# Expert blocks behind nested tests, weights read in 4096-byte runs, unused slots not gathered

## The chip, the cores and the metric

The kernel runs on one core of a Trainium2 chip. The metric is the device time of one execution in microseconds, as a median of three runs. A profile is one further execution of the same program, taken with the hardware profiler.

## The reference

One inference step of a decoder layer: a projection, two token mixers (sparse attention and gated DeltaNet), an output projection with residual, and a mixture of experts. Only the last part matters here. 1024 prompt rows and 8 sample rows each go to two of 32 experts:

```python
logit_in = jnp.take_along_axis(logit_e, grp[:, None, None], axis=1)[:, 0]
top_v, top_i = lax.top_k(logit_in, TOP_K)
weights = (p_top * jax.nn.softmax(top_v, axis=-1)).astype(h.dtype)
expert = grp[:, None] * EXPERTS_PER_GROUP + top_i
...
return (jax.nn.silu(xb @ w_gate[e]) * (xb @ w_up[e])) @ w_down[e]
...
return jnp.zeros((M, D), h.dtype).at[s_tok].add(out[dest] * s_w[:, None])
```

D is 1024, an expert is 512 wide, everything is float32. An expert's three matrices are 2 MB each, so a block of one expert reads 6.29 MB.

## The kernel before, in words

The program is a row of stages, each ended by a barrier of the engines. The three that the change touches are the last but two, the last but one and the last.

**Output projection (`block_out`, lines 2113 to 2256).** Nine tiles of rows, eight of 128 and one of 8. TensorE multiplies by `w_out`, VectorE adds the residual into `x1` and later scales it by the inverse root mean square into `h2` (line 2225), GpSimd multiplies `h2` in place by the gain (line 2256), and SP stores the tile to the DRAM table `h2_rows` (line 2143). `h2` has two buffers. A last row of zeros is stored behind the 1032 rows (line 2166); the stage ends when that has landed.

**Routing (`block_route`).** VectorE and TensorE work out which slot of which block each assignment gets. A block has 96 slots (`SLOTS`) and belongs to one expert. Blocks 0 to 31 are the first blocks of the 32 experts; an expert with over 96 rows has further blocks, numbered from 32. `tokens` holds for each slot of each block the row to gather (the row of zeros, index 1032, for an unused slot) and the row of the sample output to scatter to. The last element of `blocks` is the number n of blocks in use. Meanwhile SP loads the weights of experts 0, 1 and 2.

**Experts (`block_experts`, from line 2447).** Three weight buffers, two row buffers, two output buffers. For a block, GpSimd gathers 96 rows by an indirect DMA (line 2499), TensorE transposes them (line 2557), multiplies by gate and up weights (2567 and 2569), ScalarE and VectorE make the product (2622, 2656, 2658), TensorE transposes it (2575) and multiplies by the down weights (2587 to 2593), ScalarE and VectorE copy the result out of PSUM, and GpSimd adds it to the outputs with two accumulating indirect DMAs (line 2504), one for the prompt output and one for the sample output, each of which drops the slots that are not its own by a bounds check. SP loads the weights of block b (lines 2270 and 2273) once block b-3 has been used. The down projection of a block follows the gate and up projections of the next one. The 32 first blocks are written out. Further blocks run in a loop on each engine, six written-out bodies for each turn, each body behind a test:

```python
with engine.If(n > NE):
    with engine.Fori(0, (MAXBLK - NE) // 6) as i:
        for j in range(6):
            with engine.If(i * 6 + (NE + j) < n):
                each(i * 6 + (NE + j), ...)
```

(MAXBLK - NE) // 6 is 4. In a further block GpSimd copies the slot indices to `f_idx` first (lines 2531 and 2532), because the block's number is only in a register; and it waits for the scatters of a block before it goes on to the next. The weights' rows lie on partitions as row k * 128 + p, so a run in DRAM is one row of 512 floats, 2048 bytes; a row of the down weights has 1024 floats.

Of the kernel before, what the change touches and what calls it, by code (L numbers as in the profile page):

```python
# [17 lines left out]
ALU = mybir.AluOpType  # L18
# [3 lines left out]
P = 128  # L22
D = 1024
KD = D // P
# [21 lines left out]
MAXBLK = 56  # L46
MAXOVER = 24
# [2066 lines left out]
def block_out(nc, L, PS, C, x_p, x_s, norm_ffn, w_rg, w_re, b_rg, b_re, mixed, wo, wo_loaded, h2_rows, logits, y_p, y_s):  # L2114

    ctx = ExitStack()
    with ctx:
# [16 lines left out]
        bias = Z("o_bias", [P, NG + NE])  # L2134
        zrow = Z("o_zero", [1, D])
# [64 lines left out]
        def _(dve):  # L2200
# [10 lines left out]
            for t, n in tiles:  # L2211
# [11 lines left out]
                if t >= 2:  # L2223
                    dve.wait_ge(h2_stored[t % 2], 16 * (t // 2))
# [23 lines left out]
        def _(pool):  # L2248
            pool.wait_ge(small_loaded, 96)
            for t, n in tiles:  # L2250
# [191 lines left out]
def block_experts(nc, L, PS, C, weights, h2_rows, tokens, slot_weight, blocks, y_p, y_s):  # L2442
# [4 lines left out]
    with ctx:  # L2447
# [18 lines left out]
        def further(engine, each):  # L2466

            n = engine.value_load(blocks[0:1, MAXBLK:MAXBLK + 1], min_val=NE, max_val=MAXBLK)
            with engine.If(n > NE):
                with engine.Fori(0, (MAXBLK - NE) // 6) as i:  # L2470
                    for j in range(6):
                        with engine.If(i * 6 + (NE + j) < n):
                            each(i * 6 + (NE + j), (NE + j) % 3, j % 2, i * 2 + (NE + j) // 3 + 1, i * 3 + (NE + j) // 2 + 1)
            return n

        @block.sync
        def _(sp):
# [11 lines left out]
            def each(b, w, par, wu_count, count):  # L2489
                load(b, w, sp.value_load(blocks[0:1, bass.ds(b, 1)], min_val=0, max_val=NE - 1))  # L2490
# [4 lines left out]
        def _(pool):  # L2495
            turn, fetch = pool.alloc_register("turn"), pool.alloc_register("fetch")
# [5 lines left out]
            def scatter(par, index):  # L2502
                for c, y in enumerate((y_p, y_s)):
                    pool.indirect_dma_start(out=y, out_offset=bass.IndirectOffsetOnAxis(ap=index(c), axis=0), in_=out[par][slot, :], in_offset=None,  # L2504
                                            bounds_check=y.shape[0] - 1, oob_is_err=False, compute_op=ALU.add).then_inc(stored[par], 16)

            def scatter_first(b):
# [4 lines left out]
                scatter(b % 2, lambda c: tokens[slot, b, c:c + 1])  # L2512

            gather(0, tokens[slot, 0, 0:1])
            gather(1, tokens[slot, 1, 0:1])
            for b in range(NE):
                pool.wait_ge(xt_done, b + 1)
                gather(b % 2, tokens[slot, b + 2, 0:1])
                if b >= 1:
                    scatter_first(b - 1)  # L2520
            scatter_first(NE - 1)
            pool.wait_ge(stored[1], 32 * (NE // 2))

            def each(b, w, par, w_count, count):

                pool.reg_mov(turn, b + 1)
                done = pool.snap(turn)
                pool.reg_mov(fetch, b - (NE - 1))
                copied = pool.snap(fetch)
                pool.wait_ge(xt_done, done)  # L2530
                nc.gpsimd.tensor_copy(gidx[slot, par, :], tokens[slot, bass.ds(b + 2, 1), :].rearrange("p b c -> p (b c)")).then_inc(gidx_ready, 1)
                nc.gpsimd.tensor_copy(sidx[slot, par, :], tokens[slot, bass.ds(b, 1), :].rearrange("p b c -> p (b c)")).then_inc(sidx_ready, 1)
                pool.wait_ge(xt_done, NE)
                pool.wait_ge(gidx_ready, copied)
                gather(par, gidx[slot, par, 0:1])
                pool.wait_ge(out_act, NE)
                pool.wait_ge(sidx_ready, copied)
                pool.wait_ge(out_act, done)
                pool.wait_ge(out_dve, done)
                scatter(par, lambda c: sidx[slot, par, c:c + 1])  # L2540
                pool.wait_ge(stored[par], count * 32)
                pool.sem_inc(scattered, 1)

            n = further(pool, each)

            pool.wait_ge(x_loaded[0], (n + 1) // 2 * 16 + 16)
            pool.wait_ge(x_loaded[1], n // 2 * 16 + 16)

        @block.tensor
        def _(pe):  # L2550
            def transpose_rows(b, par, count):
                pe.wait_ge(x_loaded[par], 16 * count)
                if not (isinstance(b, int) and b < 1):
# [24 lines left out]
            def down(b, w, w_count):  # L2578
                pe.wait_ge(aT_done, b + 1)
                pe.wait_ge(d_loaded[w], 16 * w_count)  # L2580
                if not (isinstance(b, int) and b < 1):
# [24 lines left out]
            def each(b, w, par, w_count, count):  # L2606
                gate_and_up(b, w, par, w_count)
                transposes(b)
                transpose_rows(b + 2, par, count + 1)
# [169 lines left out]
```

## Time and profile before

| | us |
|---|---|
| median of 3 runs | 2648.46 (2645.39 to 2649.17) |
| the profiled execution | 2640.05 |
| its span | 2638.4 |
| TensorE matmuls busy | 2267.6 (86%) |
| weight loads into TensorE busy | 1623.9 (62%) |
| VectorE, ScalarE, GpSimd busy | 764.0, 508.3, 441.1 |
| DMA | 342.58 MB, mean 130 GB/s |

The span is the time between the first and the last instruction of the profiled execution. The page cuts it into 40 slices of 66 us. Shares are averages over stages with different limits; what the change is worth has to be read from the stage it stands in. PE is TensorE's matmuls, PEld its weight loads, DVE VectorE, ACT ScalarE, POOL GpSimd, SP the engine that issues most DMAs; a q behind a name is that engine's sequencer.

### The profile page before, as it was taken

The numbers are of one execution on the slowest core, as the hardware profiler recorded it, in microseconds if no ns is written. First come the engines' busy times: TensorE is split into PE (matmuls) and PEld (weight loads), VectorE is DVE, ScalarE is ACT, GpSimd is POOL, SyncE is SP. The second block draws the span as 40 slices with busy tenths as digits, with TensorE's granted clock in tenths as the row PEclk, the third lists the DMA queues.
The fourth block names the chain that finished last, engine by engine and source line by source line (L and its number), as shares of the span: only waits on it lengthen the run. The fifth ranks groups of instructions, "written<-read, shape, count | busy, mean of one in ns | idle before, by whom it ended". The sixth has DMA issues, their size and how long they took to land. (4 is left out here: it accounts for less than half of the span.)

```text
span 2638.4 us, 47235 instructions
## 1 busy us (share of the span) xinstructions
PE 2267.6 (86%) x20007; PEld 1623.9 (62%) x20007; DVE 764.0 (29%) x1601; ACT 508.3 (19%) x1413; POOL 441.1 (17%) x515
## 2 busy tenths in 40 slices
PE   8999998997889998798599999995899998998710
PEld 6456755886746655566466666442788787787600
DVE  2016343453656664344200000114111111111100
ACT  2111112331245555332000000101111111111100
POOL 1043121220401112102100000110122121211200
PEclk9999999997689999899699999997899999999965
DMA  5000300001200001754610000225799999999600
GB/s 169 32 32 32 137 2 1 2 2 53 50 1 2 1 1 30 199 153 128 197 47 32 32 32 17 90 80 214 281 371 358 356 368 354 369 351 361 232 13 6
DMA packets 188697, 342.58 MB, mean 130 GB/s; under 512 B 32517, under 2 KB 80142, under 8 KB 188238
## 3 DMA queue, kind: packets, MB, share of 16 engines
q1 hardware_dynamic: 166646, 305.97, 33.1%
q0 software_dynamic: 13632, 26.72, 4.0%
q10 hardware_dynamic: 8160, 6.07, 0.7%
q8 instruction: 208, 3.41, 0.6%
q14 instruction: 51, 0.42, 0.1%
HBM read 316.70 MB, written 44.55 MB: 137 GB/s over the span
## 5 line engine op out<-in xcount | busy, mean ns | idle before, releaser
L2567 PE MATMUL psum<-f_W,f_xT 128*32 128x384 f32 x3264 | 377.0, 506 | 40.2 <-DMA f_W<-w_up 37.2
L2569 PE MATMUL psum<-f_W,f_xT 128*32 128x128 f32 x3264 | 381.6, 281 | 0.1
L2569 PEld LDWEIGHTS psum<-f_W,f_xT 128*32 128x32 f32 x3264 | 365.6, 114 | 4.9 <-issue 0.3
L2083 PE MATMUL psum<-hT,x_wg 128*128 128x344 f32 x768 | 228.4, 456 | 3.3 <-DMA x_wg<-w_in 3.3
L400 PE MATMUL psum<-w,hT 128*128 128x512 f32 (+1 forms) x512 | 202.4, 553 | 0.0
L2083 PEld LDWEIGHTS psum<-hT,x_wg 128*128 128x128 f32 x768 | 147.1, 192 | 80.4 <-DMA x_wg<-w_in 3.4
L2567 PEld LDWEIGHTS psum<-f_W,f_xT 128*32 128x32 f32 x3264 | 148.1, 113 | 45.6 <-issue 37.2
L400 PE MATMUL psum<-hT,w 128*128 128x344 f32 x576 | 169.1, 454 | 0.0
L400 PEld LDWEIGHTS psum<-w,hT 128*128 128x128 f32 x512 | 96.9, 192 | 97.2 <-issue 90.4
L1620 ACT ACTIVATE a_P<-psum,a_nmax 128x512 f32<-128x512 f32 (+4 forms) x256 | 122.9, 494 | 125.1 <-DVE a_nmax L1538 84.9
L400 PEld LDWEIGHTS psum<-hT,w 128*128 128x128 f32 x576 | 108.6, 190 | 57.1 <-ACT dnT L451 0.9
L2656 DVE TENSOR_TENSOR f_a<-f_sg,psum 128x384 f32<-128x384 f32 x34 | 18.8, 554 | 413.1 <-ACT f_sg L2622 413.1
L2587 PE MATMUL psum<-f_W,f_aT 128*32 128x512 f32 x816 | 124.4, 597 | 0.7 <-DVE f_aT L2669 0.7
L2504 POOL DMA_INDIRECT out_y_prompt<-f_out,tokens x32 | 45.6, 1425 | 474.3 <-ACT f_out L2630 453.5
L2589 PE MATMUL psum<-f_W,f_aT 128*32 128x256 f32 x544 | 124.2, 382 | 0.0
L1534 DVE TENSOR_REDUCE a_nmax<-psum 128x2 f32<-128x1024 f32 (+4 forms) x128 | 91.0, 737 | 84.8 <-PE psum L1450 53.8
L2105 DVE TENSOR_TENSOR x_sig<-x_sig,psum 128x344 f32<-128x344 f32 x48 | 22.4, 508 | 318.3 <-ACT x_sig L2098 318.3
L1467 PE MATMUL psum<-constants,a_P 128*128 128x128 f32 (+1 forms) x592 | 94.7, 286 | 1.1 <-DVE a_PT L1517 0.6
L2622 ACT ACTIVATE f_sg<-psum 128x384 f32<-128x384 f32 x34 | 16.7, 490 | 395.5 <-PE psum L2569 395.5
L1447 PE MATMUL psum<-kT,qT 64*128 64x512 f32 (+3 forms) x384 | 83.0, 525 | 7.2 <-ACT a_P L1620 4.9
L2098 ACT ACTIVATE x_sig<-psum 128x344 f32<-128x344 f32 x48 | 19.3, 455 | 318.4 <-PE psum L2088 318.4
L2589 PEld LDWEIGHTS psum<-f_W,f_aT 128*32 128x32 f32 x544 | 60.0, 111 | 33.5 <-issue 0.7
(526 smaller groups left out, 3635.3 us busy)
## 6 DMA issues: line engine op xcount, KB each, us to landing
f_W<-w_gate SPq DMA_DIRECT2D x34, 2048.0 KB
f_W<-w_up SPq DMA_DIRECT2D x34, 2048.0 KB
f_W<-w_down SPq DMA_DIRECT2D x34, 2048.0 KB, 22.6
k_stage<-cache_nsa SPq DMA_DIRECT2D x128, 192.0 KB, 2.5
w<-w_in SPq DMA_DIRECT2D x6, 2048.0 KB, 7.7
x_wg<-w_in SPq DMA_DIRECT2D x8, 1024.0 KB, 10.8
x<-x_prompt SPq DMA_DIRECT2D x8, 512.0 KB, 5.4
o_w<-w_out SPq DMA_DIRECT2D x2, 2048.0 KB
```

Source lines behind the costliest of these rows:

```text
L400: ins = nc.tensor.matmul(PS[i % 4][0:m_rows, 0:n], lhsT, rhs, start=(k == 0), stop=(k == KD - 1))
L1447: ins = nc.tensor.matmul(s[:, g, col:col + w], qT[rows, j, i * P:(i + 1) * P], key, start=True, stop=not masks)
L1467: ins = nc.tensor.transpose(bank[0:keys, x * P:(x + 1) * P], Pb[u % 2][:, g, at:at + keys], C["ident"])
L1534: ins = nc.vector.tensor_reduce(stats[:, c:c + 2], S[n % 2][:, :, col:col + width(part)], AX.X, ALU.max, negate=True)
L1620: ins = nc.scalar.activation(Pb[u % 2][:, g, o:o + w], S[n % 2][:, g, col:col + w], ACT.Exp, bias=nmax[:, u % 2, c0 + g:c0 + g + 1], accum ...
L2083: ins = nc.tensor.matmul(PS[b + i][:, 0:n], wg[q % 3][:, k, i, c:c + P], hT[:, k, t0:t0 + n], start=(k == 0), stop=(k == KD - 1))
L2105: nc.vector.tensor_tensor(sg[u % 2][:, i, 0:n], sg[u % 2][:, i, 0:n], PS[4 * (u % 2) + 2 + i][:, 0:n], ALU.mult).then_inc(t_done, 1)
L2504: pool.indirect_dma_start(out=y, out_offset=bass.IndirectOffsetOnAxis(ap=index(c), axis=0), in_=out[par][slot, :], in_offset=None, bounds_ ...
L2567: nc.tensor.matmul(PS[bank][row[t], 0:NQ], xT[par][:, k, row[t]], m[:, k, 0:NQ], start=(k == 0), stop=(k == KD - 1))
L2569: ins = nc.tensor.matmul(PS[bank][row[3], P * t:P * t + P], xT[par][:, k, row[t]], m[:, k, NQ:FE], start=(k == 0 and t == 0), stop=(k == K ...
L2587: nc.tensor.matmul(PS[5][row[t], :], part(t, k), wd[w][:, k, 0:512], start=(k == 0), stop=(k == 3))
L2589: nc.tensor.matmul(PS[5][row[3], 256 * t:256 * t + 256], part(t, k), wd[w][:, k, 768:D], start=(k == 0 and t == 0), stop=(k == 3 and t == 1))
```

## The change

1. The further blocks are no longer a loop. Blocks 32 to 52 are written out, and the test for each stands inside the body of the test before it, so the first false test leaves all that follow. The block numbers are constants, and the copies of indices, the registers and their semaphores on GpSimd are gone. In a further block GpSimd gathers, scatters, and waits for both before the next block. MAXBLK goes from 56 to 53 and MAXOVER from 24 to 21.
2. Gate and up weights lie on partitions in pairs of rows: partition p gets rows k * 256 + 2p and k * 256 + 2p + 1, which is one run of 4096 bytes. The stored rows `h2_rows` are permuted to match, by GpSimd's multiply, which now reads with a step of two and writes to a buffer of its own, `h2p`. The waits for the stores move with it from VectorE to GpSimd.
3. The gathers have a bounds check: from block 2 on, an unused slot (index 1032) is out of bounds and its row is not fetched. The first two gathers still fetch the row of zeros.

```diff
-MAXBLK = 56
-MAXOVER = 24
+MAXBLK = 53
+MAXOVER = 21
...
+        h2p = Z("o_h2p", [P, 2, D])
+        by_row = lambda x: x.rearrange("p (k j r) -> p k r j", k=KD // 2, r=2)
...
-            sp.dma_start(h2_rows[t * P:t * P + n, :], h2[0:n, t % 2, :]).then_inc(h2_stored[t % 2], 16)
+            sp.dma_start(h2_rows[t * P:t * P + n, :], h2p[0:n, t % 2, :]).then_inc(h2_stored[t % 2], 16)
...
-                    dve.wait_ge(h2_stored[t % 2], 16 * (t // 2))
+                    dve.wait_ge(h2_done, t - 1)
...
-                nc.gpsimd.tensor_tensor(h2[0:n, t % 2, :], h2[0:n, t % 2, :], gain[0:n, :], ALU.mult).then_inc(h2_done, 1)
+                if t >= 2:
+                    pool.wait_ge(h2_stored[t % 2], 16 * (t // 2))
+                nc.gpsimd.tensor_tensor(h2p[0:n, t % 2, :].rearrange("p (k r j) -> p k r j", k=KD // 2, r=2), by_row(h2[0:n, t % 2, :]), by_row(gain[0:n, :]),
+                                        ALU.mult).then_inc(h2_done, 1)
...
-            queue.dma_start(dst, of(w.rearrange("e (k p) n -> e p k n", p=P), e).rearrange("a p k n -> (a p) k n")).then_inc(gu_loaded[i], 16)
+            queue.dma_start(dst.rearrange("p (k r) n -> p k (r n)", r=2), of(w.rearrange("e (k p r) n -> e p k (r n)", p=P, r=2), e).rearrange("a p k n -> (a p) k n")).then_inc(gu_loaded[i], 16)
...
-            with engine.If(n > NE):
-                with engine.Fori(0, (MAXBLK - NE) // 6) as i:
-                    for j in range(6):
-                        with engine.If(i * 6 + (NE + j) < n):
-                            each(i * 6 + (NE + j), (NE + j) % 3, j % 2, i * 2 + (NE + j) // 3 + 1, i * 3 + (NE + j) // 2 + 1)
-            return n
+            with ExitStack() as open_tests:
+                for b in range(NE, MAXBLK):
+                    open_tests.enter_context(engine.If(n > b))
+                    each(b)
...
-            def gather(par, index):
-                pool.indirect_dma_start(out=x[par][slot, :], out_offset=None, in_=h2_rows,
-                                        in_offset=bass.IndirectOffsetOnAxis(ap=index, axis=0)).then_inc(x_loaded[par], 16)
+            def gather(b):
+                pool.indirect_dma_start(out=x[b % 2][slot, :], out_offset=None, in_=h2_rows,
+                                        in_offset=bass.IndirectOffsetOnAxis(ap=tokens[slot, b, 0:1], axis=0),
+                                        bounds_check=TT if b < 2 else TT - 1, oob_is_err=False).then_inc(x_loaded[b % 2], 16)
...
-                nc.gpsimd.tensor_copy(gidx[slot, par, :], tokens[slot, bass.ds(b + 2, 1), :].rearrange("p b c -> p (b c)")).then_inc(gidx_ready, 1)
-                nc.gpsimd.tensor_copy(sidx[slot, par, :], tokens[slot, bass.ds(b, 1), :].rearrange("p b c -> p (b c)")).then_inc(sidx_ready, 1)
...
+            def each(b):
+                pool.wait_ge(xt_done, b + 1)
+                gather(b + 2)
+                scatter(b)
+                pool.wait_ge(stored[b % 2], 32 * (b // 2 + 1))
+                pool.wait_ge(x_loaded[b % 2], 16 * (b // 2 + 2))
```

The other engines' bodies change only in that block numbers and counts are constants.

## Rows read from the trace of the kernel before

**Rows 1.** The page: what the DMA engines moved in each of 40 slices.
```profile
GB/s 169 32 32 32 137 2 1 2 2 53 50 1 2 1 1 30 199 153 128 197 47 32 32 32 17 90 80 214 281 371 358 356 368 354 369 351 361 232 13 6
```

**Rows 2.** Busy time by stretches: length, engines, granted clock, DMA share, GB/s.
```profile
1876.00:1977.00 101.00, 101.00 (x1647) 86.74 (x1645) 17.03 (x34) 12.38 (x27) 19.03 (x15) 1.00 0.96 343
1977.00:2424.00 447.00, 407.90 (x6347) 353.13 (x6350) 70.44 (x142) 54.29 (x119) 89.41 (x71) 0.96 1.02 360
...
2516.20:2638.40 122.20, 0.04 (x3) 0.00 (x0) 0.85 (x2) 1.31 (x3) 2.84 (x2) 0.52 0.05 7
```

**Rows 3.** Chain and timeline: transposes of blocks 0, 6 and 31 (start, us).
```profile
1875.32 0.55 PE psum L2575 x3
...
1977.02 0.48 PE psum L2575 x3
...
2458.93 0.55 PE L2575 MATMUL psum<-constants,f_a 128*128 128x128 f32 x3
```

**Rows 4.** PE's waits, 1860 to 2460 us: total, times, longest.
```profile
PE psum L2567 <- DMA f_W<-w_up: 37.2, 16, 4.0
```

**Rows 5.** SP's last load (start, us), and its wait (total, times, longest).
```profile
2463.14 7.14 SPq L2273 DMA_DIRECT2D f_W<-w_down  x1
...
SPq L2447 <- PEq L2447: 160.8, 1, 160.8
```

**Rows 6.** DMA queues, 2516.3 to 2638.4 us: packets, MB, share of 16 engines.
```profile
q8 instruction: 48, 0.79, 4.3%
```

**Rows 7.** GpSimd's timeline in the tail: start, us, operation, idle before.
```profile
2481.96 0.18 POOL L2531 COPY f_idx<-tokens 96x2 int32 x1 [7.33 <-issue]
...
2482.95 0.96 POOL L2499 DMA_INDIRECT f_x<-h_rows,f_idx  x1 [0.69 <-issue]
...
2501.31 1.41 POOL L2504 DMA_INDIRECT out_y_sample<-f_out,f_idx  x1 [0.30 <-issue]
2504.42 0.18 POOL L2531 COPY f_idx<-tokens 96x2 int32 x1 [1.71 <-DMA out_y_sample<-f_out,f_idx]
...
2520.41 1.41 POOL L2504 DMA_INDIRECT out_y_sample<-f_out,f_idx  x1 [0.30 <-issue]
```

**Rows 8.** Weights' queue, 1832 to 1840 us, then 1842 to 1844.
```profile
q1 hardware_dynamic: 1613, 3.27, 104.9%
...
q1 hardware_dynamic: 205, 0.84, 101.9%
```

**Rows 9.** DMA queues, 1893 to 2476 us (the loaded stretch).
```profile
q1 hardware_dynamic: 78450, 189.69, 87.7%
q0 software_dynamic: 10304, 19.91, 14.1%
```

**Rows 10.** Software queue in the quiet: 2499 to 2504 us; 2504 to 2510; landing, 2482 to 2490.
```profile
DMA packets 224, 0.01 MB, mean 2 GB/s; under 512 B 222, under 2 KB 222, under 8 KB 224
...
q0 software_dynamic: 224, 0.01, 3.4%
...
q0 software_dynamic: 112, 0.39, 18.1%
...
f_x<-h_rows,f_idx POOLq DMA_INDIRECT x1, 6.0
```

**Rows 11.** Software queue beside weights, 1864 to 1866 us.
```profile
q0 software_dynamic: 115, 0.41, 84.2%
```

**Rows 12.** End of the output projection: GpSimd's last multiply by the gain.
```profile
1807.21 2.33 POOL L2256 TENSOR_TENSOR o_h<-o_h,o_gain 8x1024 f32<-8x1024 f32 x1 [0.85 <-DVE o_h L2225]
```

**Rows 13.** Routing on VectorE by line: busy us, mean ns, idle before.
```profile
L2397 DVE TENSOR_REDUCE t_ebs<-t_eb 128x24 f32<-128x768 f32 x1 | 1.0, 953 | 0.0
```

**Rows 14.** A gather in the loaded stretch, median landing, and the copy it feeds.
```profile
2209.64 0.95 POOL L2499 DMA_INDIRECT f_x<-h_rows,tokens  x1 [0.30 <-issue]
...
f_x<-h_rows,tokens POOLq DMA_INDIRECT x30, 8.4
...
2225.45 0.48 ACT L2618 COPY f_xT<-psum 128x384 f32<-128x384 f32 x1
```

More of the change, by code:

```diff
@@ L2487, in _ @@
                 load(b, b % 3, b)
[L2489 to L2490 removed]
+            def each(b):
+                load(b, b % 3, sp.value_load(blocks[0:1, b:b + 1], min_val=0, max_val=NE - 1))
             further(sp, each)
@@ L2495, in _, with scatter @@
         def _(pool):
-            turn, fetch = pool.alloc_register("turn"), pool.alloc_register("fetch")
-            def gather(par, index):
-                pool.indirect_dma_start(out=x[par][slot, :], out_offset=None, in_=h2_rows,
-                                        in_offset=bass.IndirectOffsetOnAxis(ap=index, axis=0)).then_inc(x_loaded[par], 16)
[L2502 to L2507, printed above, removed]
+            def gather(b):
+                pool.indirect_dma_start(out=x[b % 2][slot, :], out_offset=None, in_=h2_rows,
+                                        in_offset=bass.IndirectOffsetOnAxis(ap=tokens[slot, b, 0:1], axis=0),
+                                        bounds_check=TT if b < 2 else TT - 1, oob_is_err=False).then_inc(x_loaded[b % 2], 16)
+            def scatter(b):
                 pool.wait_ge(out_act, b + 1)
@@ L2511, in scatter_first @@
                     pool.wait_ge(stored[1 - b % 2], 32 * ((b - 1) // 2 + 1))
-                scatter(b % 2, lambda c: tokens[slot, b, c:c + 1])
-            gather(0, tokens[slot, 0, 0:1])
-            gather(1, tokens[slot, 1, 0:1])
+                for c, y in enumerate((y_p, y_s)):
+                    pool.indirect_dma_start(out=y, out_offset=bass.IndirectOffsetOnAxis(ap=tokens[slot, b, c:c + 1], axis=0), in_=out[b % 2][slot, :], in_offset=None,
+                                            bounds_check=y.shape[0] - 1, oob_is_err=False, compute_op=ALU.add).then_inc(stored[b % 2], 16)
@@ L2516, in _ @@
+            gather(0)
+            gather(1)
             for b in range(NE):
                 pool.wait_ge(xt_done, b + 1)
-                gather(b % 2, tokens[slot, b + 2, 0:1])
+                gather(b + 2)
                 if b >= 1:
-                    scatter_first(b - 1)
-            scatter_first(NE - 1)
+                    scatter(b - 1)
+            scatter(NE - 1)
             pool.wait_ge(stored[1], 32 * (NE // 2))
[L2524 to L2530, printed above, removed]
-                nc.gpsimd.tensor_copy(gidx[slot, par, :], tokens[slot, bass.ds(b + 2, 1), :].rearrange("p b c -> p (b c)")).then_inc(gidx_ready, 1)
-                nc.gpsimd.tensor_copy(sidx[slot, par, :], tokens[slot, bass.ds(b, 1), :].rearrange("p b c -> p (b c)")).then_inc(sidx_ready, 1)
[L2533 to L2542, printed above, removed]
@@ L2549, in _ @@
+            further(pool, each)
         @block.tensor
@@ L2552, in transpose_rows @@
                 pe.wait_ge(x_loaded[par], 16 * count)
-                if not (isinstance(b, int) and b < 1):
+                if b >= 1:
                     pe.wait_ge(xT_act, b)
@@ L2580, in down @@
                 pe.wait_ge(d_loaded[w], 16 * w_count)
-                if not (isinstance(b, int) and b < 1):
+                if b >= 1:
                     pe.wait_ge(out_act, b)
@@ L2625, in copy_out @@
                 act.wait_ge(down_done, b + 1)
-                if not (isinstance(b, int) and b < 2):
+                if b >= 2:
                     act.wait_ge(stored[par], 32 * count - 32)
@@ L2661, in copy_out @@
                 dve.wait_ge(down_done, b + 1)
-                if not (isinstance(b, int) and b < 2):
+                if b >= 2:
                     dve.wait_ge(stored[par], 32 * count - 32)
```

29 lines of the change are left out of this document (15 added, 14 removed).

## The prediction, as it went on record before the result

> **What bounds the kernel now.** I read the page first, and of it the row of GB/s in forty slices [rows 1]. It has three parts to keep apart. Up to slice 27 it mostly stands low. From slice 29 to 37 it is steady at 351 to 371 GB/s: the experts. The last two slices have 13 and 6. The change touches the last two parts and a little of the first.
>
> The table of stretches makes this exact [rows 2]. From 1876 to 1977 us PE is busy all the time. From 1977 to 2424 the DMA share is 1.02 at 360 GB/s and PE is 91% busy. From 2516.2 to the end at 2638.4 PE has nothing left. The pace of a block can be read off its transposes, one group per block [rows 3]: blocks 0 to 6 take (1977.02 - 1875.32) / 6 = 16.95 us each, blocks 6 to 31 (2458.93 - 1977.02) / 25 = 19.28 us each. So PE can do a block in 16.95 us, and over 25 blocks it loses 25 x 2.33 = 58 us. The list of waits gives 37.2 us of these to the up-projection weights [rows 4]; the rest goes with the granted clock, 1.00 in the first stretch, 0.96 in the second. Weights pace the experts.
>
> The last 122 us show up in three views. PE has no matmul behind 2516.3 [rows 2]. SP, done with its own empty tests, waits 160.8 us for PE at the block's end [rows 5]. All that the DMA queues carry after the last scatter is instruction fetches: 48 packets of 0.79 MB, 16 KB each [rows 6]. The loop of line 2472 explains it: 4 turns of 6 tests are 24 tests, of which two are true (34 blocks ran, 32 of them unconditional). So PE passes 22 bodies that it does not execute, (2638.4 - 2516.3) / 22 = 5.55 us each, about two fetches each. SP passes the same 22 from 2463.14 + 7.14 = 2470.28 to 2638.4 - 160.8 = 2477.6, or 0.33 us each: a skip costs little where the body is short and much where it is PE's.
>
> **Exit.** After the change the test of block 34 is the last that anyone makes; it is false and leaves all nineteen remaining bodies at once. PE then needs one such skip: done near 2516.3 + 5.55 = 2521.9. The next thing that is late is GpSimd. Its last scatter starts at 2520.41; the same scatter of block 32 started at 2501.31 and let GpSimd go on at 2504.42 [rows 7], 3.1 us later, so the last one lands at 2523.5. Then GpSimd leaves over nineteen written-out bodies. No row shows that jump: at least 0.3 us (SP's), at most PE's 5.55 or, should it take the fetches of two skips, 11. I take 5.5, since its nineteen bodies together are long like one of PE's and unlike SP's. With 0.3 us for the closing barrier the end is at 2529.3: **109.1 us gained** (114 to 103).
>
> **Weights in 4096-byte runs.** Gate and up weights now move in 2048 packets per block and will in 1024; down weights already move in 4096-byte packets. Undisturbed, the trace has both prices. From 1832 to 1840 the queue moved 1613 packets of 2 KB at a share of 104.9%: 1.049 x 8 us x 16 / 1613 = 83.2 ns each, 409 GB/s. From 1842 to 1844, 205 packets of 4 KB at 101.9%: 159 ns, 420 GB/s [rows 8]. Two of the small kind cost 166.4 against 159. Per block that is 1024 x 7.4 ns / 16 = 0.47 us. In the loaded stretch, 1893 to 2476, the queue's 78450 packets took 87.7% of 16 x 583 us, 104.3 ns each, for 189.69 MB or 30.15 blocks; the undisturbed mixture would be 98, so everything there costs 1.07 times as much [rows 9]. I take 0.51 us. Bounds: nothing, if the loaded stretch is held by bytes and not by packets; and 1.1 us, if the whole surplus over 98 ns went too.
>
> For that sentence of bytes there is a rule. The Trainium skill ("DMA: Bandwidth & Descriptors", section Where 436 GB/s comes from) puts about 358 GB/s as the limit of HBM for one core; the loaded stretch has 360, which fits, but the undisturbed one has 409 to 420, which does not. The same page (Why small descriptors are slow) gives a packet a fixed cost of some 3 cycles and calls joining them worthwhile only up to 256 bytes; by its cycles two 2 KB packets cost 134 against 131, an estimate of 2% of 10.6 us or 0.24 us per block. By that the sum would be some 8 us later than mine.
>
> **Unused slots.** 1032 rows go to two experts each, 2064 slots used, nearly all in the 32 first blocks, so a gather of blocks 2 to 31 drops some 32 of its 96 rows. A dropped slot is not free: the scatters show it as a small packet (those of block 32 had 222 of 224 packets under 512 B) [rows 10]. In the quiet window it cost 0.034 x 5 us x 16 / 224 = 12 ns. A gathered row costs 155 ns in the quiet (0.181 x 6 x 16 / 112), and 234 ns beside weight traffic (0.842 x 2 x 16 / 115) [rows 10, 11]. Gain per block: 32 x (155 - 33) / 16 = 0.24 at the least, where 33 ns is what the loaded stretch leaves for a small packet at 234 per large one (10304 packets, about 4860 large by their bytes, in 14.1%) [rows 9], and 32 x (234 - 12) / 16 = 0.44 at the most. I take 0.32, between the two.
>
> Together 0.83 us per block. Block time 19.28 becomes 18.45, still above PE's 16.95, so the DMA engines stay the limit and the gain passes through. Up to block 31, whose start is the last that weights hold back, some 28 loads are queued in the loaded stretch: **23 us** (bounds 7, which is 0.24 x 28 alone, and 43, worked out as rival B).
>
> **Blocks 32 and 33.** GpSimd now gathers block 34's rows right after the wait for scatter 31, without the two copies of indices: before, copy at 2481.96, gather at 2482.95, and it landed 6.0 us after its issue while PE stood [rows 7, 10]. Now all its rows are dropped, and an all-dropped scatter took 3.1 us. So some 1.3 us of copies and waits for them and 2.9 us of landing, about **4 us** gained (0 to 6). Block 33's gather hides behind gate-and-up already.
>
> **Storing the rows permuted.** GpSimd's multiply by the gain takes 2.34 us and will read with a step of two. Eight of nine run beside the next tile's matmuls on PE, which hide them; without that cover they would cost 8 x 2.3 = 18 us at twice the time. The ninth, at 1807.21, ends the stage, with only the store and the row of zeros behind it [rows 12]. No row has a stepped GpSimd read, so 0 to +2.3 us; I take **+1.2**. The moved wait (VectorE now waits for the multiply two tiles back, GpSimd for the store two tiles back) is for work of two tiles before, and costs nothing while tiles go at PE's pace.
>
> **Routing tables** of 53 columns for 56 and 21 for 24: the operations over columns of blocks lose 5%, the two over MAXOVER, 953 ns each, lose 12% [rows 13]: **-0.5**. Gathers with a bounds check may take GpSimd the 1.4 us that its scatters take, not 0.95; in the loaded stretch one starts at 2209.64, lands 8.4 us later and is wanted near 2224.5 [rows 14], so it is covered by 6 us.
>
> **Sum.** 2638.4 - 109.1 - 23 - 4 + 1.2 - 0.5 = 2503.0 us of span. The profiled execution took 2640.05, 1.65 over its span: 2504.7. The median shown is 8.4 above that execution: **2513 us**.
>
> **Rivals.** (A) The loaded stretch is held by bytes. Then 4 KB runs bring nothing and dropped rows bring their bytes, 0.131 of 6.95 MB per block, or 0.36 us: 10 us for 23, time 2526. For it: 360 GB/s is steady whatever is in the mixture. Against it: 409 to 420 when alone. The 358 GB/s of the Trainium skill, named above, would give this same time. (B) Scattered reads and short packets disturb each other more than their own durations tell; with both thinned the queue nears its undisturbed rate and PE its 16.95 us. 1536 packets of 159 ns are 15.26 us, and gathers and scatters, 2.73 us a block now (14.1% of 583 / 30.15), less 0.44: 17.55 in all, 1.73 less than now, over 25 blocks 43 us, time 2493. (C) The exit is not one jump: each of nineteen nested ends is fetched anew. Then 19 x 5.55 = 105 us come back and the time is 2618. Against it: the ends lie next to each other with no body between. This is the case in which the change does not do what it says. (D) Slower. Software packets alternate with longer weight packets on each engine, 159 for 83 ns, and gathers land late. It begins to cost when a landing grows from 8.4 to over 14.8 us [rows 14]; to be slower than before it would need 136 / 28 = 4.9 us a block more, a landing near 20 us; with 5.5 us more it is 2667. A gather puts seven packets on an engine, so alternating adds 7 x 76 ns = 0.5 us; nothing near.
>
> **Chances.** Forecast as worked out, 2502 to 2521: 0.53. A, and a late exit, 2521 to 2545: 0.22. B, with a quick exit, 2484 to 2502: 0.17. C: 0.06. D: 0.02. The range goes from 2488 to 2537, which leaves out C, D and the outer edges of A and B. Faster by over 0.2% (5.3 us, about what measurements of this kernel can tell apart) has all but D and a little of C: 0.97; same 0.01, slower 0.02.
>
> **What the new profile must show.** After the last scatter one fetch or two on PE and at most a few on GpSimd, and an end near 5 us behind it; SP's wait at the block's end short. About 1536 weight packets a block, near 165 ns each. Period of blocks 6 to 31 near 18.45 us; at 19 it is A, at 17.5 B. The wait for weights on PE below 37 us. GpSimd's multiply between 2.3 and 4.7 us. The gather of block 34 landing in about 3 us. The prediction is wrong if fetches go on after the last scatter, or if PE waits at its row transposes in every block.

## The result

The changed kernel takes 2536.77 us (4 runs, 2535.27 to 2538.57) beside 2648.1 for the kernel before: a ratio of 0.9581 [0.9565, 0.9598], 111 us faster. I had forecast 2513, 135 us faster, and my range ended at 2537; by the ratio the kernel shown with 2648.46 becomes 2537.5. The sign was right, the size was short by 24 us, just beyond the end of the range. The profiled execution took 2536.91 us.

The page of the changed kernel, the GB/s row, against [rows 1]: the two dead slices at the end are gone.

```profile
span 2535.2 us, 46962 instructions
...
GB/s 176 34 34 33 133 11 1 2 2 17 91 1 1 1 2 1 62 190 159 124 200 51 33 34 34 0 86 91 101 320 354 364 351 351 354 355 353 354 370 79
```

The stretches that answer to [rows 2], moved by the 10 us by which its experts start later:

```profile
1886.00:1987.00 101.00, 101.00 (x1647) 86.75 (x1645) 17.03 (x34) 12.41 (x27) 19.30 (x15) 1.00 0.95 342
1987.00:2434.00 447.00, 401.94 (x6337) 347.86 (x6336) 70.49 (x142) 54.43 (x119) 88.28 (x69) 0.98 1.01 355
2522.70:2535.20 12.50, 0.00 (x0) 0.00 (x0) 0.67 (x2) 1.13 (x3) 2.84 (x2) 0.67 0.04 7
```

The tail is 12.5 us for 122. The loaded stretch has hardly changed: its rate is lower (355 GB/s for 360) though each packet is now longer. The transposes of blocks 0, 6 and 31 on TensorE, from the timeline, say it in time, against [rows 3]:

```profile
1885.31 0.55 PE L2560 MATMUL psum<-constants,f_a 128*128 128x128 f32 x3 [1.76 <-DVE f_a L2643]
...
1986.93 0.33 PE L2560 MATMUL psum<-constants,f_a 128*128 128x128 f32 x1
...
2468.53 0.55 PE L2560 MATMUL psum<-constants,f_a 128*128 128x128 f32 x3
```

Blocks 6 to 31 take (2468.53 - 1986.93) / 25 = 19.26 us each; before it was 19.28, and I had forecast 18.45. TensorE's wait for up-projection weights did not shrink either, 45.9 us for the 37.2 of [rows 4]:

```profile
PE psum L2552 <- DMA f_W<-w_up: 45.9, 22, 4.4
```

Queues from 1893 to 2476 us in the changed kernel (packets, MB, share of 16 engines), to be held against [rows 9]:

```profile
q1 hardware_dynamic: 47687, 189.41, 87.1%
q0 software_dynamic: 10080, 15.38, 11.6%
```

As many bytes of weights in 0.61 of the packets took the same share of the engines' time, 170 ns a packet where I had priced 165. The software queue moves 4.5 MB less. So both changes to the traffic took place, and the time that I had expected of them did not come.

**The tail.** The rows where engines end the experts' stage (its instruction DRAIN; least, median and longest ns, all of one, then its start), first of the kernel before, then of the changed one:

```profile
L2447 SPq DRAIN  x1: 7/7/7, 2477.5 to 2477.5; - x1
L2447 POOLq DRAIN  x1: 4882/4882/4882, 2531.1 to 2531.1; - x1
L2447 PEldq DRAIN  x1: 13/13/13, 2638.1 to 2638.1; - x1
```

```profile
L2452 PEldq DRAIN  x1: 67/67/67, 2524.6 to 2524.6; - x1
L2452 POOLq DRAIN  x1: 4947/4947/4947, 2530.0 to 2530.0; - x1
```

TensorE, at its drain 107 us behind GpSimd's before, is now there 2.1 us after its last matmul. GpSimd ends the kernel, with a drain of 4.9 us that was there before too, under TensorE's cover. From the last scatter to the end it is 2535.2 - 2526.38 = 8.8 us, for 2638.4 - 2520.41 = 118.0: **109.2 us, where I had forecast 109.1**. But that last scatter itself comes 6 us later than before, and I had expected it 26 us earlier.

**Where those went.** Lined up on GpSimd's work, the changed kernel is already 12.6 us behind before the first changed instruction: the first multiply by the gain starts at 1675.7 us, for 1663.1. No line of the stages up to there had been edited.

### The profile page after: what moved, and what is told of

Read it like the earlier page. It is cut to its first block and busy times, and to the rows that moved or that the text cites. A ratio compares the mean times of both kernels' runs of the same rounds, so it can differ in the third digit from the quotient of the medians.

```text
span 2535.2 us, 46962 instructions
## 1 busy us (share of the span) xinstructions
PE 2269.1 (90%) x20007; PEld 1625.7 (64%) x20007; DVE 764.3 (30%) x1601; ACT 509.1 (20%) x1413; POOL 447.1 (18%) x511
## 5 line engine op out<-in xcount | busy, mean ns | idle before, releaser
L2552 PE MATMUL psum<-f_W,f_xT 128*32 128x384 f32 x3264 | 369.5, 499 | 46.8 <-DMA f_W<-w_up 45.9
L2554 PE MATMUL psum<-f_W,f_xT 128*32 128x128 f32 x3264 | 374.2, 278 | 0.0
L2098 ACT ACTIVATE x_sig<-psum 128x344 f32<-128x344 f32 x48 | 19.3, 454 | 319.7 <-PE psum L2088 319.7
```

Of the source, the lines that this page charges most:

```text
L2552: nc.tensor.matmul(PS[bank][row[t], 0:NQ], xT[par][:, k, row[t]], m[:, k, 0:NQ], start=(k == 0), stop=(k == KD - 1))
L2554: ins = nc.tensor.matmul(PS[bank][row[3], P * t:P * t + P], xT[par][:, k, row[t]], m[:, k, NQ:FE], start=(k == 0 and t == 0), stop=(k == K ...
```

## The experiments

All ratios are to the kernel before on the same chip, with 95% intervals. In the tables, "ahead" is the start of GpSimd's first multiply by the gain, "route" the time from SP's first expert load to the first gather, "block" the mean of blocks 6 to 31, "last" the time between the Silu of blocks 31 and 33 on ScalarE, "tail" the time from the start of the last scatter to the end of the span; all are from the profiled execution's timeline, in us. A difference of 0.1 us in "block" says nothing: the kernel before itself has 19.28 and 19.42 in two profiles.

**First, the parts apart, on one chip.** `e1_exit_only` is the changed kernel with the weights' runs, the order of the stored rows and the gathers as before; `e2_runs_2k` undoes the runs and the order of the rows alone, `e3_gather_all` the dropped slots alone, `e4_after_again` nothing. Lines are shortened with `...`.

```diff
 e1, e2
-        by_row = lambda x: x.rearrange("p (k j r) -> p k r j", k=KD // 2, r=2)
+        by_row = lambda x: x
...
-                nc.gpsimd.tensor_tensor(h2p[0:n, t % 2, :].rearrange("p (k r j) -> p k r j", k=KD // 2, r=2), by_row(h2[0:n, t % 2, :]), by_row(gain[0:n, :]),
+                nc.gpsimd.tensor_tensor(h2p[0:n, t % 2, :], by_row(h2[0:n, t % 2, :]), by_row(gain[0:n, :]),
...
-            queue.dma_start(dst.rearrange("p (k r) n -> p k (r n)", r=2), of(w.rearrange("e (k p r) n -> e p k (r n)", p=P, r=2), e)...
+            queue.dma_start(dst, of(w.rearrange("e (k p) n -> e p k n", p=P), e)...
 e1, e3
-                                        bounds_check=TT if b < 2 else TT - 1, oob_is_err=False)...
+                                        bounds_check=TT, oob_is_err=False)...
```

> The changed kernel with 2048-byte runs, rows stored unpermuted, and all 96 slots of every block gathered: of the change only the exit, the constants in place of the loop and the smaller tables are left. Exit theory: after the last matmul about 10 us to the end, where the kernel before has 122, so 109 us gained there and 3 to 4 in blocks 32 and 33: 112 faster than before, near 2536. Theory P (packet and slot prices hold in the loaded stretch and the changed kernel's 12 us of drift in the stages ahead hid them): this one is 13 to 23 us slower than the changed kernel, near 2555. Theory Z (neither the runs nor the dropped slots give anything in the loaded stretch): same as the changed kernel within 3 us, and blocks 6 to 31 at 19.2 to 19.3 us each.

> The changed kernel with 2048-byte runs and rows stored unpermuted; slots are dropped as in the changed kernel. Theory P, with packets priced by duration: 13 us slower than the changed kernel. Packets priced by throughput in the quiet window (1613 in 8 us against 205 in 2 us, 158.7 against 156.1 ns for 4 KB): 5 us slower. Theory Z: no difference within 3 us. A fourth outcome, that long packets hurt the software queue: this one faster than the changed kernel.

> The changed kernel with 4096-byte runs, but unused slots gathered as before. Theory P: 7 to 12 us slower than the changed kernel. If the loaded stretch is held by bytes: 10 us slower. Theory Z: no difference within 3 us.

> The changed kernel as it is, beside the three on one chip. Shows how far a second execution of one program moves: GpSimd's first multiply by the gain at 1663 us in the profile before and 1676 in that of the changed kernel, with nothing changed ahead of it. Theory of chance (stages ahead vary by execution): some other start than 1676, with the time moving alike. Theory of layout (the changed program itself slows the stages ahead): 1676 again, and 1663 in the kernel before.

| | us | ratio | ahead | route | block | last | tail |
|---|---|---|---|---|---|---|---|
| before (profile shown) | | | 1663.1 | 37.3 | 19.28 | 53.8 | 118.0 |
| e1: exit alone | 2558.93 | 0.9665 [0.9645, 0.9684] | 1672.0 | 39.0 | 19.92 | 53.4 | 8.9 |
| e2: exit, dropped slots | 2555.49 | 0.9637 [0.9612, 0.9663] | 1670.6 | 39.8 | 19.69 | 51.4 | 9.2 |
| e3: exit, long runs | 2542.74 | 0.9600 [0.9580, 0.9620] | 1670.3 | 32.7 | 19.42 | 52.7 | 8.8 |
| e4: all three | 2532.22 | 0.9562 [0.9542, 0.9581] | 1672.2 | 32.8 | 19.15 | 50.5 | 8.8 |

Theory Z falls: the runs are worth 16 to 23 us and both together 27 us, about what I had forecast for them. The dropped slots give 10 us beside long runs (e3 to e4); the 3 us beside short ones (e1 to e2) are not clear of noise, since e2's five runs lie between 2544 and 2558. What is short is the exit alone: 92 us, although its tail has given back 109 in every one of these profiles. In e1 the same traffic as before takes 19.92 us a block in place of 19.28, and the stages ahead are 9 us late. Something in the written-out kernels slows them, or the profile before was a quick execution.

**Is it the form, and is it the check?**

> The kernel before, profiled once more. In the four profiles so far of programs with the exit, GpSimd's first multiply by the gain starts at 1670 to 1676 us, in the profile before at 1663; and the one with all of the old traffic took 19.92 us per block where the profile before has 19.28. If that profile was a quick execution (theory of chance): now the first multiply at 1670 or later, 19.6 us or more per block, span near 2650 or above. If the written-out form itself costs time (theory of form): 1663 and 19.3 again.

> The first experiment (exit alone, 2048-byte runs, all slots gathered) with its gathers as in the kernel before, with no bounds check at all. If the check as such costs time in the loaded stretch: 19.3 us per block in place of 19.92 and 15 us less in all, 2544. If not: within 3 us of the first experiment's 2559.

> The kernel before, with a bounds check on all of its gathers that drops nothing. If the check as such costs: 10 to 16 us slower than before. If not: same within 3 us.

```diff
 e5 (on e1)
-                                        bounds_check=TT, oob_is_err=False).then_inc(x_loaded[b % 2], 16)
+                                        ).then_inc(x_loaded[b % 2], 16)
 b2 (on the kernel before)
+                                        in_offset=bass.IndirectOffsetOnAxis(ap=index, axis=0), bounds_check=TT, oob_is_err=False)
```

| | us | ratio | ahead | route | block | tail |
|---|---|---|---|---|---|---|
| b1: before again | 2652.46 | 1.0010 [0.9997, 1.0022] | 1664.6 | 38.1 | 19.42 | 118.3 |
| b2: before, check | 2650.95 | 1.0003 [0.9992, 1.0014] | 1668.0 | 38.3 | 19.35 | 118.2 |
| e5: e1, no check | 2562.99 | 0.9674 [0.9652, 0.9695] | 1671.8 | 39.0 | 19.96 | 9.0 |

The kernel before keeps its 19.3 to 19.4, the written-out one its 19.9. So it is not chance, and the check has no part in it. A small group of DMAs far ahead of the experts shows the slowing most plainly, since no other load runs beside it: the compression weights (`h_wg`, 8 loads of 256 KB in packets of 256 bytes, lines unchanged). From 400 to 700 us, first the kernel before, then the changed one; the last number of the load's row is the median landing:

```profile
q1 hardware_dynamic: 14368, 6.64, 8.8%
...
h_wg<-w_cmp SPq DMA_DIRECT2D x8, 256.0 KB, 4.9
```

```profile
q1 hardware_dynamic: 14368, 6.64, 10.9%
...
h_wg<-w_cmp SPq DMA_DIRECT2D x8, 256.0 KB, 6.8
```

The same packets and bytes, a quarter more engine time. I used this landing as the mark in what follows.

**Is it the program's length?** No.

> The first experiment (exit alone) with nested tests for blocks 32 to 37 only, six bodies as in the kernel before; nothing is left out for these inputs, which use 34 blocks. Theory of size: the twenty-one bodies make the program longer, and a longer program's DMAs run slower everywhere (the compression weights land 6.8 us after issue where they took 4.9, 19.92 us per block where it was 19.35 to 19.42). Then 19.4 us per block, first multiply by the gain at 1664 to 1668 us, and some 20 us less than the first experiment, near 2537. Rival, theory of form (constants in place of registers, or the smaller tables, cost the time): 2557 as in the first experiment.

> The changed kernel with nested tests for blocks 32 to 37 only (enough for these inputs). Theory of size: 15 to 20 us less than the changed kernel's 2532, near 2515, which is the prediction's figure; 18.7 us per block. Theory of form: same as the changed kernel.

> The kernel before with fifteen further bodies written out behind its loop on all engines but GpSimd, inside a test that is never true. Theory of size: the DMAs slow down as in the written-out kernels, 19.9 us per block and the first multiply at 1670 or later, plus one more skip on TensorE (5.5 us): 2670 to 2677. Theory of form: the skip alone, 2656.

> The first experiment (exit alone) with a DRAM table of rows that is 16 MB longer, the added rows never touched. If what counts is where tensors lie in DRAM, and the program's length only moves them, this may move them as well: some time other than 2559, by more than 4 us either way. If the length itself counts: 2559.

```diff
 e7 (on e1), e8 (on the changed kernel)
-                for b in range(NE, MAXBLK):
+                for b in range(NE, NE + 6):
 b4 (on the kernel before, behind the loop, all engines but GpSimd)
+            if not pool_engine:
+                with engine.If(n > MAXBLK - 1):
+                    for j in range(15):
+                        each(NE + j, (NE + j) % 3, j % 2, (NE + j) // 3 + 1, (NE + j) // 2 + 1)
 e9 (on e1)
-    h2_rows = nc.dram_tensor("h2_rows", [TT + 1, D], F32, kind="Internal").ap()
+    h2_rows = nc.dram_tensor("h2_rows", [TT + 1 + 4096, D], F32, kind="Internal").ap()[0:TT + 1, :]
```

| | us | ratio | ahead | block | tail | `h_wg` landing |
|---|---|---|---|---|---|---|
| e7: e1, six bodies | 2559.96 | 0.9647 [0.9623, 0.9671] | 1674.6 | 20.04 | 8.6 | 7.0 |
| e8: changed, six bodies | 2533.53 | 0.9564 [0.9542, 0.9586] | 1674.3 | 19.27 | 8.8 | 6.9 |
| b4: before, dead code | 2654.57 | 1.0027 [1.0014, 1.0040] | 1665.5 | 19.35 | 123.8 | 5.0 |
| e9: e1, longer table | 2562.90 | 0.9673 [0.9657, 0.9689] | 1669.5 | 19.93 | 9.2 | 6.7 |

My theory of size fell in all four, and so did the thought of where tensors lie in DRAM (e9). One thing came out of b4 beside it: a single further false test over a long body on TensorE lengthened the tail from 118.3 to 123.8 us, 5.5 us, just the price per skip that the prediction had worked out.

**Is it the tables?** The change makes MAXBLK 53. Its tables are narrower, and I had costed that in the prediction as -0.5 us of VectorE.

> The first experiment (exit alone) with MAXBLK 56 and MAXOVER 24 as in the kernel before, so 24 bodies written out. Theory of tables (the narrower table of constants, or what it moves in DRAM, slows the DMAs): compression weights land at 4.9 us, 19.4 us per block, about 15 to 20 us less than the first experiment, 2540. Theory of tests (nested tests in place of loops do it): 2559.

> The changed kernel with MAXBLK 56 and MAXOVER 24. Theory of tables: 2515, blocks of 18.7 us. Theory of tests: the changed kernel's 2533.

> The kernel before with MAXBLK 50 and MAXOVER 18: three turns of the loop for four, 16 bodies skipped for 22, so 6 x 5.55 = 33 us off the tail. The inputs need 34 blocks, so nothing is left out. Theory of tables: DMAs slow as in the written-out kernels, 19.9 us per block, 2617 + 18 = 2635. Theory of tests: 2617, blocks of 19.4 us.

> The kernel before with nested written-out tests on TensorE only; the other engines keep their loops, and the tables their size. The tail falls to what the next slowest engine needs for its 22 skips; SP needs 0.33 us each, GpSimd is not known. If nested tests on TensorE slow the DMAs: 19.9 us per block. If they don't: blocks of 19.4 us, and up to 109 us off, near 2541, if GpSimd skips as cheaply as SP.

```diff
 f1 (on e1), f2 (on the changed kernel)
-MAXBLK = 53
-MAXOVER = 21
+MAXBLK = 56
+MAXOVER = 24
 f3 (on the kernel before)
-MAXBLK = 56
-MAXOVER = 24
+MAXBLK = 50
+MAXOVER = 18
 f4 (on the kernel before)
+        def further_out(engine, each):
+            n = engine.value_load(blocks[0:1, MAXBLK:MAXBLK + 1], min_val=NE, max_val=MAXBLK)
+            with ExitStack() as open_tests:
+                for b in range(NE, MAXBLK):
+                    open_tests.enter_context(engine.If(n > b))
+                    each(b, b % 3, b % 2, b // 3 + 1, b // 2 + 1)
...
-            further(pe, each)
+            further_out(pe, each)
```

| | us | ratio | ahead | route | block | last | tail | `h_wg` |
|---|---|---|---|---|---|---|---|---|
| f1: exit alone, 56 | 2537.14 | 0.9564 [0.9543, 0.9585] | 1669.3 | 37.7 | 19.40 | 53.5 | 9.3 | 5.0 |
| f2: changed, 56 | 2520.97 | 0.9518 [0.9494, 0.9543] | 1665.4 | 33.2 | 19.00 | 50.2 | 9.0 | 5.0 |
| f3: before, 50 | 2637.42 | 0.9949 [0.9928, 0.9969] | 1671.5 | 39.3 | 19.96 | 54.3 | 84.6 | 6.9 |
| f4: exit on TensorE | 2547.04 | 0.9603 [0.9583, 0.9623] | 1669.2 | 38.1 | 19.38 | 53.7 | 15.3 | 4.9 |

It is the tables, in both directions. f3 is the sharpest: six skips fewer take 33.7 us off the tail, 5.6 each, and the kernel is only 14 us faster, because its blocks now take 19.96 us. f2 stayed short of what I expected of it, 2515 and blocks of 18.7 us; that comes back below. (In f4 GpSimd ends the kernel: it needs 7.1 us for its own 22 skips and then drains.)

**Which of the two things that the tables move?** A table of constants is loaded from DRAM and has one column per block number: 2425 columns, now 2422. On the chip everything is laid out behind it:

```python
A_OB = A_CONST + ((CONST.shape[1] * 4 + 31) // 32) * 32
A_R = A_OB + DH * TT * 4
...
W = [L.at(f"f_W{i}", A_R + 49152 * i, [P, 3 * 4096]) for i in range(3)]
```

2425 columns are 9700 bytes, rounded to 9728; 2422 are 9688, rounded to 9696. With A_CONST at 16512 + 33024, the weight buffers start at 75776 in each partition in the kernel before, a multiple of 512, and at 75744 in the changed one, 32 bytes past a multiple of 64. All that lies behind moves with them: `h_wg` from 190976, again a multiple of 512, to 190944. In the tables the weight buffers' address stands for all.

> The changed kernel, MAXBLK 53, with the region behind the table of constants rounded up to a multiple of 64 bytes for 32: the buffers lie where they lie in the kernel before (75776), the table in DRAM stays narrow. Theory of the buffers' address: 2519 to 2523 as with MAXBLK 56, compression weights landing in 4.9 us, blocks of 19.0 us. Theory of the DRAM table: 2532 to 2537 as in the changed kernel, 6.9 us.

> The same with everything behind the table 64 bytes higher still (75840: a multiple of 64, not of 128 or 256). If a multiple of 64 is enough: 2521. If DMAs want a multiple of 128 or 256: 2532 or slower, compression weights landing near 6.9 us.

```diff
 g1 (on the changed kernel; g2 adds 64 more)
-A_OB = A_CONST + ((CONST.shape[1] * 4 + 31) // 32) * 32
+A_OB = A_CONST + ((CONST.shape[1] * 4 + 63) // 64) * 64
```

| | buffers at | us | ratio | ahead | route | block | last |
|---|---|---|---|---|---|---|---|
| e4: changed kernel | 75744 | 2532.22 | 0.9562 [0.9542, 0.9581] | 1672.2 | 32.8 | 19.15 | 50.5 |
| g1: rounded to 64 | 75776 | 2521.80 | 0.9512 [0.9496, 0.9528] | 1662.7 | 32.8 | 19.01 | 50.1 |
| g2: 64 higher | 75840 | 2533.81 | 0.9549 [0.9535, 0.9563] | 1671.6 | 32.7 | 19.25 | 50.8 |

The mark for g1, then for g2, same stretch and columns as above:

```profile
q1 hardware_dynamic: 14368, 6.64, 8.7%
...
h_wg<-w_cmp SPq DMA_DIRECT2D x8, 256.0 KB, 4.9
```

```profile
q1 hardware_dynamic: 14368, 6.64, 10.5%
...
h_wg<-w_cmp SPq DMA_DIRECT2D x8, 256.0 KB, 6.8
```

So it is where the buffers lie on the chip, not the table in DRAM; and a multiple of 64 is not enough, 75840 is as slow as 75744. g1 and g2 ran on one chip and differ in nothing else: 12.0 us.

On 128 the profiles say something, though no run was made for it. The gate weights of the stage before the output projection (`x_wg`, loads of 1 MB in packets of 1 KB) go to three buffers in turn. The first starts at 75776, the second and third at 157824 and 174208, which are multiples of 128 and not of 256. Three microseconds with the queue full, 2.7 us behind the issue of the fourth pair of loads, which goes to the first buffer; the kernel before (1393.1 to 1396.1 us), then the changed one (1405.7 to 1408.7):

```profile
q1 hardware_dynamic: 1146, 1.16, 108.8%
```

```profile
q1 hardware_dynamic: 1091, 1.10, 109.0%
```

And 6.9 us behind the issue of the third pair, when packets for the second buffer pass; the same two kernels (1321.6 to 1324.6 and 1334.2 to 1337.2 us):

```profile
q1 hardware_dynamic: 1034, 1.04, 110.0%
```

```profile
q1 hardware_dynamic: 1035, 1.04, 110.0%
```

In all eight profiles with the weight buffers at 75776 the first count is 1128 to 1149, in the twelve others 1085 to 1095; the second is 1033 to 1039 in all twenty. A shift costs the buffer that started at a multiple of 256 its speed, and does nothing to the one that started 128 past such a multiple. So 128 seems not to be enough; but the second buffer is slower in either place than the first one shifted, so something else may hold that stretch and hide the address. 256 and 512 are not told apart by any run.

The Trainium skill has a rule near this ("DMA: Bandwidth & Descriptors", How a descriptor splits into AXI transactions): a transaction that reads must start at a multiple of 256 bytes, and a descriptor that does not start there fetches, and pays for, the bytes from the multiple below it. The rule is told of reads, and the addresses moved here are written to. The traces agree that addresses off such multiples are slower; they do not follow the rule's amounts, if it held for writes, by which 64 past a multiple of 256 (75840) should cost less than 224 past it (75744): `h_wg` lands in 6.8 us at either.

g1 is, level with f2, the best kernel here: 131.9 us below the kernel before on its chip.

**What holds the blocks once the buffers are in place?** f1 and f2 differ in the runs and the dropped slots together, and only by 0.40 us a block. The stretches of blocks 6 to 31 in f1, f2 and e1 (columns as in [rows 2]) have, as their last number, the rate in GB/s:

```profile
1983.40:2468.40 485.00, 442.49 (x6876) 383.31 (x6875) 74.62 (x150) 57.08 (x125) 95.94 (x75) 0.96 1.02 359
1976.30:2451.30 475.00, 436.32 (x6876) 377.64 (x6875) 74.62 (x150) 57.08 (x125) 95.94 (x75) 0.97 1.00 361
1987.20:2485.10 497.90, 446.08 (x6876) 386.91 (x6876) 74.57 (x150) 57.06 (x125) 95.93 (x75) 0.95 1.02 353
```

With the buffers in place this rate is 358 to 362 GB/s in all eight profiles, six of them with short runs and two with long ones. Out of place it is 349 to 353 with short runs and 355 to 360 with long ones. So with the buffers in place the stretch looks held by bytes, as rival A had it, and the dropped rows alone would give 0.36 us a block. No run undoes the runs alone with the buffers in place, so what long runs give there is not shown.

**The barrier behind routing.** The tables also show "route" 5 to 7 us shorter wherever runs are long. The drains at the end of routing tell why. The kernel before:

```profile
L2285 ACTq DRAIN  x1: 824/824/824, 1844.2 to 1844.2; - x1
L2285 SPq DRAIN  x1: 123/123/123, 1849.2 to 1849.2; - x1
```

The changed kernel:

```profile
L2290 ACTq DRAIN  x1: 812/812/812, 1856.9 to 1856.9; - x1
L2290 SPq DRAIN  x1: 123/123/123, 1857.4 to 1857.4; - x1
```

Before, SP came 5.0 us after ScalarE; now 0.5. It issues nine loads of 2 MB, and behind the first ones an issue keeps it for up to 7.4 us. Before, the third issue already took 3.5 us; with long runs it took 0.5. I read that as a queue with room for so many packets, so that with half the packets more bytes fit; no row shows the queue's room. `e6_last_load_later` tests whether SP's issuing holds the barrier, on e1, by one load that is issued behind it:

```diff
                 load_gate_and_up(sp, e, e)
-                load_down(sp, e, e)
+                if e < 2:
+                    load_down(sp, e, e)
...
+            load_down(sp, 2, 2)
             for b in range(3, NE):
```

> The first experiment (2048-byte runs, all slots gathered) with the third expert's down weights issued at the start of the experts' stage and not at the end of routing. In its profile SP reaches the barrier behind routing at 1859.8, ScalarE at 1852.7; with 4096-byte runs SP is there at 1854.0. Theory: SP's issuing holds that barrier, since an issue waits for room in the queue. Then SP gets there at 1853.8, the first gather starts 6 us sooner after the first load, and the time falls by 4 to 6 us. Rival: the 6 us are swallowed by the weights, which pace the stage behind: first gather sooner, time unchanged.

Its drains:

```profile
L2290 ACTq DRAIN  x1: 812/812/812, 1854.8 to 1854.8; - x1
L2290 SPq DRAIN  x1: 123/123/123, 1855.9 to 1855.9; - x1
```

Route is 33.4 us, for 39.0 in e1 and e5. The time is 2556.75, ratio 0.9645 [0.9629, 0.9661], 6 us below e5 on the same chip (0.9674 [0.9652, 0.9695]). The intervals overlap, so that the time follows is likely and not shown; that SP's issuing held the barrier is shown: ScalarE now comes 1.1 us before it, for 7.1 in e1.

## Why the prediction was wrong, step by step

**Exit: right, to 0.1 us**, in size. One cause in it was not: I gave GpSimd 5.5 us for jumping over nineteen bodies. It gets to the block's end 3.6 us after its scatter starts and then drains for 4.9. I had 3.1 + 5.5 + 0.3 us behind the scatter, and it was 3.6 + 4.9 + 0.3: that the parts meet at the same end is luck. Of the 16 KB fetches in queue q8 one is left:

```profile
q0 software_dynamic: 224, 0.04, 3.2%
q14 instruction: 3, 0.02, 0.7%
q8 instruction: 1, 0.02, 0.5%
```

These are the queues of the changed kernel from 2522.7 us on; [rows 6] has 48 such fetches.

**Routing tables, "-0.5": this is the step that failed.** I costed the narrower tables by the VectorE operations that read them, and did not follow the size of the constants into the addresses of everything placed behind them. What it measured: 12.0 us on one chip, g1 against g2; by e4 against g1 and by ratio 0.0050 of 2650, 13 us; by f1 against e1, with short packets, 0.0101, 27 us. 6 us of it lie ahead of the change: the first multiply starts at 1666.0 us on average in the eight profiles with buffers at 75776 (1662.7 to 1669.3) and at 1672.3 in the twelve others (1669.5 to 1675.7). The rest is in the experts.

**Weights in long runs and unused slots, 23 us: right in sum only because of that failure.** With the buffers in place the two together give 19.40 - 19.00 = 0.40 us a block (f1 to f2), not 0.83: 10 us over blocks 6 to 31. So this term was mis-sized by half; which part of it, no run shows, and two workings give the measured number. One is the packet's price. I took share x time / packets, but the share in those windows was 104.9 and 101.9%: packets overlap, and short ones more. By what passed in the time, 8 x 16 / 1613 = 79.4 ns and 2 x 16 / 205 = 156.1, two short packets cost 158.7 against 156.1, so 0.17 us a block and not 0.47 [rows 8]; with 0.24 for the slots, my lower bound, that is 0.41. The other is rival A: long runs bring nothing and the dropped bytes 0.36, and the rate of 358 to 362 GB/s in place, whatever the runs, speaks for it. With buffers out of place the two changes give 19.92 - 19.15 = 0.77, since short packets suffer more there. (My upper bound for long runs, 1.1 us, was mis-added as well: by its own terms, 2560 packets of 104.3 ns against 1536 of 159, it is 1.4.) The quiet window at the same distance from the first load, 8 us from 1833.5 in b1, then from 1840.9 in e1, has 5.5% fewer short packets:

```profile
q1 hardware_dynamic: 1614, 3.27, 105.0%
```

```profile
q1 hardware_dynamic: 1526, 3.09, 104.3%
```

**Not in my sum at all: the barrier behind routing**, 5 us, won by the long runs.

**Blocks 32 and 33, 4 us: right.** "Last" falls from 53.8 to 50.7 with the change, and from 55.5 in b1 to 50.1 in g1. The gather of block 34 lands in 2.1 us, for 6.0 [rows 10]; its timeline row in the changed kernel is

```profile
2493.43 1.00 POOL L2500 DMA_INDIRECT f_x<-h_rows,tokens  x1 [7.54 <-issue]
```

**Storing the rows permuted, +1.2: right within its bounds.** The stepped read costs 2.81 us for 2.34, so +0.5 at the stage's end:

```profile
L2260 POOL TENSOR_TENSOR o_h2p<-o_h,o_gain 128x1024 f32<-128x1024 f32 (+1 forms) x9 | 25.3, 2806 | 7.8 <-DVE o_h L2227 7.8
```

**The sum again**, with what was measured, from b1 to g1, spans of 2647.7 and 2514.8: tail 109.5, blocks 6 to 31 10.2, route 5.3, blocks 31 to 33 5.4, block 33 to the last scatter 2.3, ahead 1.9, less 1.8 in between: 132.8 of 132.9 us. I had forecast 135.5. By g1's ratio the kernel of the prediction's figures would be at 0.9512 x 2648.46 = 2519. The remaining 18 us up to 2537 are the buffers' addresses, as well as measurements on different chips can tell: the direct comparisons give 12 and 13.

**The rivals.** A (bytes hold the stretch), with a late exit, has the time of the result, 2521 to 2545, and is not why the kernel missed 2519: the exit was not late, and with the same bytes e2 is 23 us slower than e4, and g2 12 us slower than g1. For what was left to gain with the buffers in place it may well hold, as said. B did not come. C is excluded by the tail, D by the waits: TensorE waits 11.9 us for gathered rows from 1860 to 2470, nearly all of it once at the start.

## What to carry to other kernels

A size that is changed moves everything laid out behind it: before and after an edit, print the start addresses of the buffers that DMAs fill, and round regions up to the alignment that the fast ones had. A drift that starts ahead of the first edited instruction is a finding and not noise, once it comes back in a second profile; a small DMA with nothing beside it, in a stage that no one edited, makes a good mark for it. Price packets by how many pass in a time, not by how long each is open, and look at the rate of the loaded stretch in several runs before you count on fewer packets. Code that is skipped costs where its body is long, and a loop's empty turns pay for it each time: leave by one test.

## What the runs showed of the hardware

- Buffers 32 bytes below or 64 above a multiple of 512 in each partition (75744 or 75840 for 75776, and `h_wg` likewise) made DMAs into them slower: 6.8 us to land a 256 KB load of 256-byte packets for 4.9, 5.5% fewer 2 KB packets in 8 us of a quiet stretch, 0.15 to 0.24 us more per block with 4 KB packets (19.15 and 19.25 for 19.00 and 19.01) and 0.5 with 2 KB (19.92 for 19.40).
- The same shift did nothing to a buffer that started 128 past a multiple of 256: 1034 and 1035 packets of the queue in 3 us.
- With buffers in place the loaded stretch moved 358 to 362 GB/s, with 2 KB as with 4 KB packets; in the quiet, [rows 8] give 409 and 420.
- A false test over a long body on TensorE costs 5.5 us: 5.55 in the kernel before, 5.5 for one more in b4, 5.6 for each of six fewer in f3. Over all nineteen at once it took 2.1 us at most. On SP it costs 0.33.
- GpSimd's drain at the end of the experts' stage, behind its indirect DMAs, takes 4.9 us.
- An indirect DMA of which all rows are dropped lands in 2.1 us, one of 96 rows in 6.0.
- SP is kept by the issue of large loads, up to 7.4 us for one of 2 MB behind others: half as many packets let it go 5 us earlier from nine of them.
